# Later sines, squares summed on GpSimd, joined gate weights and paired bias blocks in a hybrid decoder trunk

## The chip, the cores and the metric

The kernel runs on one core of one Trainium2 chip. The metric is the device time of one execution in microseconds, lower is better. The engines are named as the profile names them: PE (TensorE, with PEld for its weight loads), DVE (VectorE), ACT (ScalarE), POOL (GpSimd) and SP (SyncE, which here only issues transfers).

## What is computed

The reference is a trunk of two layers over 512 tokens of width 2048, all in float32. Each layer normalises its input, multiplies it with one combined input projection, feeds the slices to three mixers, gates each, and adds the output projection:

```python
for layer in range(DEPTH):
    xn = rms_norm(h, norm_g[layer])
    mem_kv = mem_n @ mem_w_kv[layer]
    if layer % 2 == 0:   # S5 state-space mixer | forgetting attention | memory attention
        mixed = even_layer(xn, mem_kv, even_w_in[i], s5_lam_re[i], ..., fox_b_f[i])
    else:                # latent attention | sparse attention | memory attention
        mixed = odd_layer(xn, mem_kv, positions, t5_table, odd_w_in[i], ...)
    h = h + (mixed @ w_out[layer]).astype(h.dtype)
return rms_norm(h, final_norm_g)
```

Four pieces matter here. The S5 mixer turns its parameters into a complex decay (`mag * cos(li * dt)`, `mag * sin(li * dt)`) and a factor divided by `lr * lr + li * li`. The forgetting attention has eight forget gates, `log_sigmoid(f_logit + b_f)`, whose logits are eight columns of the input projection. The latent attention normalises two latents of 512 rows: `rms_norm(c_q, g_cq)` and `rms_norm(c_kv, g_ckv)`, which needs the sum of squares over 512 channels for each token. The sparse attention adds a position bias, `t5_table[bucket(distance)]`, to its scores.

## The kernel before, in words

All large products are one list of jobs (`plan`), worked through in order by five instruction streams that are written out by hand and meet only at semaphores. A job is cut into chunks of 512 columns and a chunk into slots of two contraction tiles. For each slot SP loads 512 KB of weights into one of four buffers `wraw` (line 175; it may do so once DVE is done with the slot four before), ACT rounds them to the matmul's type (`act_slot`, line 188), DVE computes what rounding lost (`dve_slot`, line 192), and PE multiplies: high by high, high by low and low by high, three matmuls for each tile and bank (`pe_part`, line 223). So a slot of a full job is 24 matmuls of 512 columns. The ring `wsp` has four slots as well: ACT may convert slot n once PE is done with slot n - 4. Results of a chunk stay in PSUM banks 0 to 3; ACT copies them to `stage` and stores them (`act_evac`, line 303, store at line 343). That evacuation stands in ACT's order after three slots of the next chunk have been converted, and the next chunk's first matmul waits for the banks.

The jobs at the start are memk0, memv0, memk1, memv1 (keys and values of the memory, from `mem`), then E0, E1 and E2 (the even layer's input projection), then GLU. The memk jobs have 256 token columns. E2 is the job of the eight forget-gate columns: its slot is six matmuls whose stationary operand is 128x8. Small work is hooked in between slots: `hook(s)` runs after slot s on each engine.

**The start.** POOL loads the rows of `x` (line 2348) once the first job's transposes are done, then the S5 parameters (`pool_prep_loads`, lines 596 to 603), and runs a long chain of small steps on them (`pool_prep`, lines 611 and 614). In the middle POOL waits for two sines from ACT (`act_prep_sin`, lines 694 and 695) and one reciprocal from DVE (`dve_prep_den`, line 699). ACT and DVE come to these after the conversions of memk1; both stand ahead of the conversions of memv1. PE transposes the results in chunk 1 of E0 (`pe_prep`, line 706). Meanwhile the transposes of x's normalised rows (`pe_tile`, line 472), their scaled copies by ACT (`act_tile`, line 388) and low parts by DVE (`dve_tile`, line 457) are hooked into memk1 and memv1.

**The forget gates.** E2's bank is evacuated after three slots of GLU have been converted. The logits go to DRAM, back to SBUF (`flS`), and through `act_forget` and `dve_forget`, which stand after GLU's conversions.

**The attention sequences.** `Seq` lays the softmax units of a layer (`seq_scores`, `seq_max`, `seq_exp`, `seq_norm`, ...) in steps x, with the matmuls of the output projection filled in between, and `splits` says at which step ACT and DVE convert which slot of that projection.

**The position bias.** The odd layer's bias is built in 32 blocks n while job O1's chunks 1 to 4 run: DVE compares (`dve_t5_ind`), PE multiplies after slot n (`pe_t5`, lines 1897 and 1898), ACT copies (`act_t5_row`), POOL stores (`pool_t5_out`). A block is twelve matmuls with 32 stationary columns each, going to the four partition groups of one bank, three over the same columns, and one 128x128 matmul with an identity that adds the mask. The block's width is 128, 256, 384 or 512 columns, eight blocks of each.

**The latents' squares.** In chunk 6 of O1, ACT squares eight tiles (`act_c`, line 2022), and PE sums each over its partitions with a matmul of ones, two after each of the slots 2 to 5 (`pe_c`, line 2068, float32). ACT's third square waits for the first of these matmuls.

## Time and profile before

| | us |
|---|---|
| median of three runs | 2368.56 |
| lowest and highest | 2366.68, 2369.6 |
| the profiled execution | 2363.92 |
| its span in the profile | 2362.2 |
| PE busy in the span | 2305.3 |
| DVE, ACT, POOL busy | 997.5, 826.4, 374.1 |

The page cuts the span into 40 slices, and its row of the granted clock shows 9 (full) in all but the second. 345.6 MB are moved at 146 GB/s on average. A row of the timeline gives the start and the length of a run of like instructions, their count, and in brackets how long the engine had sat idle before it and who ended that.

### The profile page before, as it was taken

The page shows a single profiled execution, that of the slowest core. Times are in us where ns is not written, and L with a number is a line of the kernel's source. Part 1 is how long each engine was busy: PE and PEld are TensorE (multiplying, and loading weights), DVE is VectorE, ACT ScalarE, POOL GpSimd, SP SyncE. Part 2 cuts the span into 40 slices and gives each one's busy share as a digit, 9 for nine tenths or more (in the row PEclk, how much of TensorE's full clock was granted, in tenths as well). Part 3 has the DMA queues.
Part 4 walks back from the last instruction along what each step waited for, and adds up shares of the span by engine and source line. Part 5 has one row for each costly group of instructions (what it writes and reads, how often), then busy time and mean ns, then how long its engine had stood idle before and what let it go on. Part 6 is the DMA issues. An engine that isn't in the chain of part 4 may idle for free.

```text
span 2362.2 us, 30631 instructions
## 1 busy us (share of the span) xinstructions
PE 2305.3 (98%) x11817; PEld 1873.8 (79%) x11817; DVE 997.5 (42%) x1862; ACT 826.4 (35%) x1468; POOL 374.1 (16%) x629
## 2 busy tenths in 40 slices
PE   7899999999999999999999999999999999999998
PEld 6788888888888877888877777788888866778887
DVE  4533444544432246553353442351121345666534
ACT  5433323333332434432342222322222443455323
POOL 2814111111110011210010001000000154121100
PEclk9899999999999999999999999999999999999999
DMA  8544434444345245654344446345442664454532
GB/s 278 183 127 143 124 110 111 115 125 117 106 124 190 72 140 196 203 178 141 98 147 136 129 140 220 111 121 156 138 121 71 220 222 148 153 181 140 205 116 97
DMA packets 165610, 345.60 MB, mean 146 GB/s; under 512 B 20743, under 2 KB 31319, under 8 KB 163043
## 3 DMA queue, kind: packets, MB, share of 16 engines
q1 hardware_dynamic: 106944, 188.51, 26.5%
q0 software_dynamic: 29840, 98.42, 13.2%
q10 hardware_dynamic: 28691, 56.82, 6.6%
q8 instruction: 91, 1.49, 0.3%
q14 instruction: 44, 0.36, 0.0%
HBM read 279.88 MB, written 63.82 MB: 145 GB/s over the span
## 4 chain that ended last, share of the span: by engine, by line
PE 93%; POOL 2%; DVE 1%; issue 1%; ACT 1%; DMA 1%; SPq 0%; DVEq 0%; ACTq 0%; POOLq 0%
PE PS L223 75%; PE PS L1583 3%; PE PS L2212 2%; PE PS L1572 1%; PE PS L2084 1%; PE PS L271 1%; POOL S L614 1%; PE PS L2109 1%; PE PS L1013 1%; PE PS L1009 1%; PE PS L472 1%; POOL S L611 1%; PE PS L1897 1%; PE PS L1332 1%; PE PS L2105 1%
## 5 line engine op out<-in xcount | busy, mean ns | idle before, releaser
L223 PE MATMUL PS<-A,wsp 128*128 128x512 f32 (+1 forms) x5232 | 1175.4, 384 | 2.5 <-ACT stage L303 1.2
L223 PEld LDWEIGHTS PS<-A,wsp 128*128 128x128 f32 x5232 | 946.4, 187 | 199.0 <-issue 3.7
L192 DVE TENSOR_TENSOR wsp<-wraw,wsp 128x1024 fp32r<-128x1024 f32 (+2 forms) x366 | 435.8, 1192 | 1114.3 <-ACT wsp L188 1113.1
L223 PE MATMUL PS<-wsp,A 128*128 128x512 f32 x2976 | 765.4, 402 | 15.5 <-DVE wsp L192 12.4
L188 ACT ACTIVATE wsp<-wraw 128x1024 fp32r<-128x1024 f32 (+2 forms) x366 | 374.2, 1025 | 996.4 <-PE PS L223 960.3
L223 PEld LDWEIGHTS PS<-wsp,A 128*128 128x128 f32 x2976 | 542.3, 190 | 120.0 <-DVE wsp L192 13.1
L303 ACT ACTIVATE stage<-PS 128x512 f32<-128x512 f32 (+1 forms) x150 | 87.0, 586 | 131.4 <-PE PS L223 131.2
L1619 ACT ACTIVATE S<-PS 128x256 f32<-128x256 f32 (+3 forms) x160 | 63.1, 394 | 129.8 <-PE PS L1572 128.9
L1583 PEld LDWEIGHTS PS<-S 128*128 128x128 f32 x640 | 93.4, 192 | 12.0 <-issue 2.4
L1627 ACT ACTIVATE S<-PS,stats 128x256 f32<-128x256 f32 (+3 forms) x160 | 74.8, 468 | 74.1 <-DVE stats L1664 61.7
L1583 PE MATMUL PS<-S 128*128 128x128 f32 x640 | 95.5, 276 | 1.2 <-issue 1.1
L1572 PE MATMUL PS<-ident,S 128*128 128x128 f32 x336 | 64.4, 277 | 2.3 <-ACT S L1619 2.2
L1572 PEld LDWEIGHTS PS<-ident,S 128*128 128x128 f32 x336 | 45.0, 148 | 20.7 <-issue 10.5
L1664 DVE CUSTOM_DVE_ANT_0 PS<-PS,S 128x512 f32<-128x512 f32 (+4 forms) x80 | 34.9, 437 | 44.1 <-PE PS L1465 23.1
L1914 POOL DMA_DIRECT2D biasD<-S x32 | 17.5, 548 | 226.6 <-ACT S L1908 218.8
L388 ACT ACTIVATE A<-PS,gcol 128x512 fp32r<-128x512 f32 (+1 forms) x48 | 27.6, 613 | 61.9 <-PE PS L472 61.9
L457 DVE SCALAR_TENSOR_TENSOR A<-PS,gcol,A 128x512 fp32r<-128x512 f32 (+1 forms) x48 | 30.1, 657 | 44.2 <-ACT A L388 43.8
L797 POOL COPY S<-S 64x64 f32<-64x64 f32 x32 | 11.9, 401 | 216.6 <-PE PS L959 216.1
L1885 DVE TENSOR_SCALAR S<-S 128x128 bf16<-128x128 f32 (+3 forms) x128 | 40.6, 382 | 0.0
L1678 DVE TENSOR_SCALAR S<-S,stats,gtm 128x32 f32<-128x32 f32 (+4 forms) x96 | 38.3, 399 | 4.1
L810 POOL DMA_DIRECT2D kD<-S x64 | 33.6, 554 | 32.7 <-DVE S L907 29.6
L815 POOL DMA_DIRECT2D S<-kD x64 | 33.6, 534 | 12.9 <-DMA kD<-S 12.8
(326 smaller groups left out, 1741.1 us busy)
## 6 DMA issues: line engine op xcount, KB each, us to landing
wraw<-in_even_w_in_dram SPq DMA_DIRECT2D x112, 512.0 KB, 3.7
wraw<-in_odd_w_in_dram SPq DMA_DIRECT2D x88, 512.0 KB, 3.6
wraw<-in_w_out_dram SPq DMA_DIRECT2D x80, 512.0 KB, 3.7
wraw<-in_mem_w_kv_dram SPq DMA_DIRECT2D x32, 512.0 KB, 4.7
yO<-stage ACTq DMA_DIRECT2D x12, 1024.0 KB
yE<-stage ACTq DMA_DIRECT2D x10, 1024.0 KB
S<-yO POOLq DMA_DIRECT2D x36, 256.0 KB, 3.6
hA<-stage ACTq DMA_DIRECT2D x8, 1024.0 KB
```

Source lines behind the costliest of these rows:

```text
L188: nc.scalar.activation(wsp[:, q, 0, :, 0:j["cols"]], wraw[:, q, :, 0:j["cols"]], ACT.Copy).then_inc(w_hi, 1)
L192: nc.vector.tensor_tensor(wsp[:, q, 1, :, 0:j["cols"]], wraw[:, q, :, 0:j["cols"]], wsp[:, q, 0, :, 0:j["cols"]].bitcast(F32), ALU.subtrac ...
L223: mm = nc.tensor.matmul(dst, lhs, rhs, start=(s == 0 and kk == 0 and i == 0), stop=(s == j["spc"] - 1 and kk == 1 and i == 2))
L303: nc.scalar.activation(stage[0:rows, f, 0:n], PS[0:rows, f, 0:n], func, scale=scale).then_inc(banks_free, 1)
L1572: mm = nc.tensor.transpose(PS[:, 6, j_ * P:j_ * P + P], seqP[x % 4][:, j_ * P:j_ * P + P], ident[:, :])
L1583: mm = nc.tensor.matmul(PS[:, 7, i * P:i * P + P], u["v"](j_), seqT[x % 2][:, j_ * P:j_ * P + P], start=(j_ == 0 and u["first"]), stop=(j_ ...
L1619: nc.scalar.activation(seqT[x % 2][:, 0:n], PS[:, 6, 0:n], ACT.Copy).then_inc(a_ev, 1)
L1627: nc.scalar.activation(seqP[c][:, 0:w], PS[:, 4 + x % 2, 0:w], ACT.Exp, bias=stats[:, 4 + c:5 + c], scale=-1.0 if u["bias"] is not None el ...
L1664: nc.vector.tensor_tensor_reduce(bank, bank, u["bias"], -1.0, 3e38, ALU.add, ALU.min, accum_out=top).then_inc(a_mx, 1)
L1678: nc.vector.tensor_scalar(p, p, stats[:, 12 + c:13 + c], u["gate"], ALU.mult, ALU.mult).then_inc(a_nr, 1)
L1885: nc.vector.tensor_scalar(indS[n % 4][j_][:, 0:w], poskS[:, 0:w], atS[:, 4 * n + j_:4 * n + j_ + 1], None, ALU.is_le).then_inc(t5_ind, 1)
L2212: return nc.tensor.matmul(bank[:, 0:w], nsaQ[r][:, i * P:i * P + P], keys[which][:, 0:w], start=True, stop=True)
```

## The change

- **Start.** POOL waits for x's row block 1 before it issues the S5 parameter loads. `act_prep_sin` and `dve_prep_den` move from behind memk1's conversions to behind those of E0's chunk 0.
- **Forget gates.** The low halves of the eight weight columns are put beside the high halves (columns 8 to 15 of one operand), so that one matmul yields both products; the slot falls from six matmuls to four, the job from 48 to 32. The result has 16 rows, stored and loaded as two groups of eight, which DVE adds (`f_part`) before ACT's `act_forget` may start.
- **Latents.** ACT writes the first square of each latent to `sqA[g]` and the others to two buffers; POOL adds them up (`pool_c_squares`, six additions, behind `pool_w1(1)` in its order and ahead of `pool_w2`); PE sums each latent with one matmul, after slots 4 and 6. Two matmuls of ones instead of eight.
- **Bias blocks.** `pe_t5` does two blocks after each odd slot instead of one after each slot; the identity matmul is cut into four of 32 columns. ACT's row copies come one slot later.
- **Sequences.** The conversions in `splits` begin two steps later (at step 3 instead of 1).

```diff
@@ dve_slot
-            nc.vector.tensor_tensor(wsp[:, q, 1, :, 0:j["cols"]], wraw[:, q, :, 0:j["cols"]],
+            low = wsp[:, q, 0, :, 8:16] if j is E2 else wsp[:, q, 1, :, 0:j["cols"]]
+            nc.vector.tensor_tensor(low, wraw[:, q, :, 0:j["cols"]],
@@ new, in place of pe_chunk(pe, E2, 0)
+        def pe_forget_gates(pe):
+            pe.wait_ge(banks_free, E2["first_free"][0])
+            for s, n, q, r, early in chunk_slots(E2, 0):
+                pe.wait_ge(w_lo, n + 1)
+                for kk in range(2):
+                    kt = 2 * s + kk
+                    for low in (kt > 0, kt == 0):
+                        rows, ap = (8, E2["lo"]) if low else (16, E2["hi"])
+                        mm = nc.tensor.matmul(PS[0:rows, 0, :], wsp[:, q, 0, kk, 0:rows], A[:, ap + kt, :], start=(kt == 0 and not low),
+                                              stop=(kt == KD - 1 and not low))
+                mm.then_inc(slot_used, 1)
@@ act_forget
-            act.wait_ge(fin_, 32)
+            act.wait_ge(f_part, 1)
@@ dve_forget
             dve.wait_ge(fin_, 32)
+            nc.vector.tensor_tensor(flS, flP[:, 0], flP[:, 1], ALU.add).then_inc(f_part, 1)
+            dve.wait_ge(f_part, 1)
@@ Seq
-                self.splits, at = {}, 0
+                self.splits, at = {}, 2
@@ pe_t5
-        def pe_t5(pe, n):
...
+        def pe_t5(pe, n0):
+            for n in (n0, n0 + 1):
...
+                for i in range(3):
+                    for j_ in range(4):
+                        nc.tensor.matmul(bank[32 * j_:32 * j_ + 32, 0:w], dB[i], indS[n % 4][j_][:, 0:w], start=(i == 0), stop=False)
                 for j_ in range(4):
-            nc.tensor.matmul(bank[:, w - P:w], identB, mixB[:, 112 - 16 * g:240 - 16 * g], start=False, stop=True).then_inc(t5_pe, 1)
+                    rows = slice(32 * j_, 32 * j_ + 32)
+                    mm = nc.tensor.matmul(bank[rows, w - P:w], identB[:, rows], mixB[:, 112 - 16 * g:240 - 16 * g], start=False, stop=True)
+                mm.then_inc(t5_pe, 1)
@@ act_c
-                    if k >= 2:
-                        act.wait_ge(ss_pe, k - 1)
-                    nc.scalar.activation(sqS[k % 2], cS[:, k, :], ACT.Square).then_inc(sq_ok, 1)
+                    g, i = k // 4, k % 4
+                    if 3 * g + i - 1 >= 2 and i:
+                        act.wait_ge(sq_added, 3 * g + i - 2)
+                    nc.scalar.activation(sqS[(3 * g + i - 1) % 2] if i else sqA[g], cS[:, k, :], ACT.Square).then_inc(sq_ok, 1)
+        def pool_c_squares(pool):
+            for g in range(2):
+                for i in range(1, 4):
+                    pool.wait_ge(sq_ok, 4 * g + i + 1)
+                    if i > 1:
+                        pool.wait_ge(sq_added, 3 * g + i - 1)
+                    nc.gpsimd.tensor_tensor(sqA[g], sqA[g], sqS[(3 * g + i - 1) % 2], ALU.add).then_inc(sq_added, 1)
@@ pe_c
-            if 2 <= s < 6:
-                if s == 2:
...
+            if s in (4, 6):
+                g = s // 2 - 2
...
+                pe.wait_ge(sq_added, 3 * g + 3)
+                nc.tensor.matmul(PS[:, 6 + g, :], ones[:, :], sqA[g], start=True, stop=True).then_inc(ss_pe, 1)
@@ gpsimd
+            pool.wait_ge(rows_in[1], 16)
             pool_prep_loads(pool)
...
-            pool.dma_start(flS, yE[7168:7176, :]).then_inc(fin_, 16)
+            pool.dma_start(flP, yF.rearrange("g r t -> r g t")).then_inc(fin_, 16)
...
             pool_w1(pool, 1)
+            pool_c_squares(pool)
@@ scalar (and the like for dve_prep_den on vector)
-                if n_ == 2:
-                    act_prep_sin(act)
             act_chunk(act, E0, 0, pend, lambda s: act_early(act, 4, s))
+            act_prep_sin(act)
...
-lambda s: act_t5_row(act, 8 * c + s - 13) if 0 <= 8 * c + s - 13 < 32 else None)
+lambda s: act_t5_row(act, 8 * c + s - 14) if 0 <= 8 * c + s - 14 < 32 else None)
@@ tensor
-            pe_chunk(pe, E2, 0)
+            pe_forget_gates(pe)
...
-                pe_chunk(pe, O1, c, lambda s: pe_t5(pe, 8 * (c - 1) + s))
+                pe_chunk(pe, O1, c, lambda s: pe_t5(pe, 8 * (c - 1) + s - 1) if s % 2 else None)
```

## Rows read from the trace of the kernel before

**Rows 1.** The page: busy us, share of the span, instructions of each engine

```profile
PE 2305.3 (98%) x11817; PEld 1873.8 (79%) x11817; DVE 997.5 (42%) x1862; ACT 826.4 (35%) x1468; POOL 374.1 (16%) x629
```

**Rows 2.** Waits of PE, whole span: total us, times, longest us

```profile
PE PS L223 <- DVE wsp L192: 13.4, 3, 8.8
```

**Rows 3.** Timeline of PE, 42 to 112 us: start, length, work, [idle before]

```profile
42.77 13.79 PE L223 MATMUL PS<-wsp,A 128*128 128x512 f32 x60
...
60.17 10.08 PE L223 MATMUL PS<-wsp,A 128*128 128x512 f32 x36 [3.61 <-DVE wsp L192]
...
70.93 14.30 PE L223 MATMUL PS<-A,wsp 128*128 128x256 f32 x117 [0.34 <-ACT stage L303]
...
95.01 0.60 PE L472 MATMUL PS<-ident,S 128*128 128x128 f32 x4
...
104.45 4.66 PE L223 MATMUL PS<-wsp,A 128*128 128x512 f32 x12 [8.84 <-DVE wsp L192]
...
109.30 3.00 PE L223 MATMUL PS<-wsp,A 128*128 128x512 f32 x12
```

**Rows 4.** Windows: stretch, length, engines busy, PEclk, DMA share, GB/s

```profile
60.20:61.00 0.80, 0.80 (x2) 0.71 (x3) 0.00 (x0) 0.55 (x2) 0.40 (x2) 0.51 1.04 381
```

**Rows 5.** Timeline of ACT and POOL over the same stretch

```profile
85.71 0.69 ACT L388 ACTIVATE A<-PS,gcol 128x512 fp32r<-128x512 f32 x1 [2.19 <-PE PS L472]
...
98.80 0.31 ACT L694 ACTIVATE S<-S 32x128 f32<-32x128 f32 x1 [11.10 <-POOL S L611]
...
103.76 1.15 ACT L303 ACTIVATE stage<-PS 128x256 f32<-128x256 f32 x4
...
120.12 0.52 POOL L611 TENSOR_SCALAR S<-S 32x128 f32<-32x128 f32 x1
```

**Rows 6.** Timeline, PE's transposes of S5 parameters in chunk 1 of E0

```profile
188.35 0.68 PE L706 MATMUL PS<-ident,S 32*128 32x32 f32 x8
```

**Rows 7.** DMA queues, 40 to 44 us: packets, MB, share of 16 engines

```profile
q0 software_dynamic: 201, 1.52, 96.8%
```

**Rows 8.** DMA queues, 48 to 52 us

```profile
q0 software_dynamic: 126, 0.39, 53.7%
q1 hardware_dynamic: 128, 0.23, 34.9%
```

**Rows 9.** Timeline, PE early in the second attention sequence

```profile
2010.28 0.49 PE L2212 MATMUL PS<-A 128*128 128x128 f32 x2 [2.50 <-ACT S L1627]
```

**Rows 10.** Groups of PE by shape, 837 to 848 us: busy, mean ns

```profile
L223 PE MATMUL PS<-A,wsp 128*8 128x512 f32 x48 | 11.0, 389 | 0.0
```

**Rows 11.** Timeline, 847 to 889 us, all engines

```profile
847.20 1.06 ACT L188 ACTIVATE wsp<-wraw 128x1024 fp32r<-128x1024 f32 x1 [0.53 <-DMA wraw<-in_s_w_glu_dram]
...
848.16 0.57 ACT L303 ACTIVATE stage<-PS 8x512 f32<-8x512 f32 x1
...
848.88 43.77 PE L223 MATMUL PS<-A,wsp 128*128 128x512 f32 x192 [0.99 <-DVE wsp L192]
...
886.16 2.35 DVE L192 TENSOR_TENSOR wsp<-wraw,wsp 128x1024 fp32r<-128x1024 f32 x2
```

**Rows 12.** Windows, 842 to 844 us, columns as in rows 4

```profile
842.00:844.00 2.00, 2.00 (x10) 0.79 (x9) 0.33 (x2) 0.22 (x1) 0.55 (x1) 1.00 1.04 363
```

**Rows 13.** Chain that ended last, 1495 to 1525 us: start us, us, what

```profile
1499.34 5.49 PE PS L223 x24
...
1504.83 1.72 PE PS L2068 x4
```

**Rows 14.** The same chain, a stretch of plain matmuls

```profile
1520.96 70.77 PE PS L223 x312
```

**Rows 15.** The same chain at a block of 512 columns, 1417 us

```profile
1417.38 0.76 PE PS L1897 x12
...
1418.30 5.54 PE PS L223 x24
```

**Rows 16.** Line 1897: idle of PE's weight loads before it (us, times)

```profile
  issue: 11.3, 32
```

More of the change, by code:

```diff
@@ L301, in act_evac @@
                 n = j["n"] if j["mode"] == "F" else COLS
-                rows = min(P, j["cols"])
+                rows = 16 if j is E2 else min(P, j["cols"])
                 nc.scalar.activation(stage[0:rows, f, 0:n], PS[0:rows, f, 0:n], func, scale=scale).then_inc(banks_free, 1)
@@ L1886, in dve_t5_ind @@
                                         ALU.is_le).then_inc(t5_ind, 1)
-        def pe_t5(pe, n):
-            w, g = (n // 8 + 1) * P, n % 8
-            bank = PS[:, 4 + n % 4, :]
-            pe.wait_ge(t5_ind, 4 * n + 4)
-            if n >= 4:
-                pe.wait_ge(t5_row, 2 * (n - 3))
-            for i in range(3):
+        def pe_t5(pe, n0):
+            for n in (n0, n0 + 1):
+                w, g = (n // 8 + 1) * P, n % 8
+                bank = PS[:, 4 + n % 4, :]
+                pe.wait_ge(t5_ind, 4 * n + 4)
+                if n >= 4:
+                    pe.wait_ge(t5_row, 2 * (n - 3))
+                for i in range(3):
+                    for j_ in range(4):
+                        nc.tensor.matmul(bank[32 * j_:32 * j_ + 32, 0:w], dB[i], indS[n % 4][j_][:, 0:w], start=(i == 0), stop=False)
                 for j_ in range(4):
-                    nc.tensor.matmul(bank[32 * j_:32 * j_ + 32, 0:w], dB[i], indS[n % 4][j_][:, 0:w], start=(i == 0), stop=False)
-            nc.tensor.matmul(bank[:, w - P:w], identB, mixB[:, 112 - 16 * g:240 - 16 * g], start=False, stop=True).then_inc(t5_pe, 1)
+                    rows = slice(32 * j_, 32 * j_ + 32)
+                    mm = nc.tensor.matmul(bank[rows, w - P:w], identB[:, rows], mixB[:, 112 - 16 * g:240 - 16 * g], start=False, stop=True)
+                mm.then_inc(t5_pe, 1)
         def act_t5_row(act, n):
@@ L1924, in build @@
         rrS = [PS[:, 6 + r, :] for r in range(2)]
+        sqA = [S[:, 10240 + 512 * r:10752 + 512 * r] for r in range(2)]
+        sq_added = sem("sq_added")
         w2S = S[:, 4096:4608].rearrange("p (k h d) -> p k h d", k=2, h=2)
@@ L2061, in pe_c @@
         def pe_c(pe, s):
-            if 2 <= s < 6:
-                if s == 2:
+            if s in (4, 6):
+                g = s // 2 - 2
+                if g == 0:
                     pe.wait_ge(t5_row, 64)
-                for k in (2 * s - 4, 2 * s - 3):
-                    pe.wait_ge(sq_ok, k + 1)
-                    nc.tensor.matmul(PS[:, 6 + k // 4, :], ones[:, :], sqS[k % 2], start=(k % 4 == 0), stop=(k % 4 == 3)).then_inc(ss_pe, 1)
+                pe.wait_ge(sq_added, 3 * g + 3)
+                nc.tensor.matmul(PS[:, 6 + g, :], ones[:, :], sqA[g], start=True, stop=True).then_inc(ss_pe, 1)
         W1_AT = (2, 6, 10, 14, 18, 22, 26, 30)
```

14 lines of the change are left out of this document (8 added, 6 removed).

## The prediction, as it was made before the result

> **What bounds the kernel now.** I read the page first: PE is busy for 2305.3 of 2362.2 us [rows 1]. So a part of the change can only pay in two ways: it takes instructions off PE, or it closes one of the few holes in PE's work. The waits of PE say where the holes are: 13.4 us in all go to conversions that came late, 8.8 of them at one place [rows 2]. The timeline of PE shows the places, both at the start [rows 3]. One is a hole of 3.61 us before 60.17 in memv0; the other opens when the transposes at 95.01 end (95.61) and closes at 104.45, in front of memv1. Each is paid twice: 12 matmuls take 4.66 us behind the second and 3.00 a slot later, and 36 take 10.08 behind the first, where 60 took 13.79 (so 8.3) before it. The windows give the reason: right after the first hole the granted clock is 0.51, the 1.2 GHz level of the two [rows 4]. Everywhere else a plain slot follows a plain slot, and a part is worth what it takes out of PE's stream.
>
> **1. The sines.** ACT sat idle for 11.10 us before the first sine at 98.80, because POOL was still preparing the angle; behind the sine stood the conversions of memv1 and the evacuation of memk1 [rows 5]. The change takes this wait out of memv1's way. What is late next? PE's matmuls of memv1 want memk1's first bank, which ACT frees after the scaled copy of the last transposed tile (0.69 us) and one bank's copy (1.15 / 4 = 0.29) [rows 5]. So PE stands still for about 1.0 us after 95.61 and starts at 96.6. One slot (12 matmuls at 13.79 / 60 = 0.23, so 2.8 us) and the transposes (0.60 busy, about 0.45 of PE's time) bring its second slot to 99.8, where before it came at 109.5 (the row at 109.30, less what matmuls overlap) [rows 3]. Gain 9.7 us; 8.8 if the low clock came nonetheless for half its time, 10.5 if the copies run ahead.
>
> The moved work: two sines of 0.3 us with a table load on ACT, one reciprocal on DVE, and the rest of POOL's chain, which took from 98.80 to 120.64, 22 us, partly waiting for DVE [rows 5]. They now come about when PE is in slot 4 of E0's first chunk, near 157 on the old scale; POOL ends by 180 at the latest, and PE wants the result at 188.35 [rows 6]. ACT and DVE are three slots ahead of PE there. Cost nothing; if POOL took 10 us longer than before, the rest would show in full. POOL's later constants load sits behind this chain, and nobody asks for it before the odd layer.
>
> **2. The S5 loads behind x.** The hole before 60.17 is a transfer's. x's rows hold the 16 DMA engines at 96.8% from 40 to 44 us [rows 7], and then the S5 loads take 53.7% of them for only 0.39 MB in 4 us, while SP's weights get 34.9% and 0.23 MB [rows 8]: small pieces are slow, and a 0.52 MB slot that starts there takes many microseconds. The change starts the S5 loads only when x has landed, some 3 to 4 us after the bus is free for weights. In that time at the rate of [rows 7] (1.52 / 4 = 0.38 MB per us) two weight slots land, and these are the two that memv0's hole waited for. So the hole of 3.61 and its 1.8 us of slow clock (10.08 - 8.3) go [rows 3]. But the bytes remain, and the engines were full until about 63: the third slot of memk1, behind which ACT frees memv0's banks, lands near 65.5 by the same sum of bytes. With its conversion (1.06) and a bank's copy memk1 starts at about 67.9, not at 70.93. Gain 3.0 us. Bounds: 5.4 (both costs gone, nothing late) and -1.8 (the new wait of some 2.5 us before memk1 as long as the old, and the clock falls there too). The nearest hole on PE without low clock is 2.50 us [rows 9], so I leave the clock out.
>
> **3. The forget gates.** 16 of 48 matmuls go: 11.0 / 48 x 16 = 3.7 us of PE [rows 10]. Do they reach the end? Behind them GLU starts at 848.88. ACT converts three GLU slots first; the third waited for its transfer (0.53 us) until 847.20, then came the evacuation of E2's bank, 0.57 us, which releases PE [rows 11]. Between 842 and 844 the DMA engines are full, 1.04 at 363 GB/s [rows 12]: they carry these slots as fast as they can, and the store of the previous chunk ahead of them doesn't move. So E2 would end 3.7 us sooner and GLU start almost when it did: I take 0.3 us. PE's hole there grows from 0.99 to about 4.4 us, longer than the one of 3.61 behind which 1.8 us were lost to the clock [rows 3]. Sum -1.5 us. Bounds +3.7 (everything reaches the end) and -3.3 (low clock for twice as long). The new add on DVE puts ACT's gate chain about 2 us later. It ends in GLU's sigmoids and DVE's conversions of the output job, done at 888.5, while PE is in GLU until 892.6 [rows 11]: hidden, with 4 us of cover, of which it takes up to 2.
>
> **4. The latents.** Between 1499.34 and 1506.55 lie 24 plain matmuls and two with ones, which add 1.72 us in the chain [rows 13]; six of the eight go: 6 x 0.86 = 5.2 us. ACT's squares no longer wait for PE but for POOL, which is idle then; its additions are of the size of one ACT copy, PE needs them a slot or more later. Taken at full value; bounds 3.5 (each of PE's two waits 0.9 late) and 5.5.
>
> **5. The bias blocks.** A plain matmul costs 70.77 / 312 = 0.227 us, so 0.443 ns per column [rows 14]. A block of 512 columns costs 0.92 us from 1417.38 to 1418.30, and the 24 matmuls behind it 5.54 instead of 24 x 0.227 = 5.44 [rows 15]: 1.02 us. Its columns are 3 x 512 + 128, or 0.74 us. The rest, 0.28, is not stream: the weight loads sit idle 11.3 / 32 = 0.35 us before each block, with no releaser [rows 16]. I read this as the cost of changing between 128 and 32 stationary columns. Before, each block changes over twice (into it, and from its twelve matmuls to the identity); now a pair does so twice, half as often. Gain 32 x 0.28 / 2 = 4.5 us. Bounds: 5.6 (the whole 0.35 at 16 visits) and -0.9, if the four quarters of the identity run one after the other (3 x 128 columns, 0.17 us, 32 times = 5.4 us) rather than side by side, as the twelve do. If each quarter cost a share of its own as an instruction, it would be at most 0.76 / 12 = 0.063 us [rows 15].
>
> The Trainium skill ("TensorEngine Tiling (Array Packing)", Instruction Overhead) speaks against the quarters: each matmul has about 60 cycles of overhead. At 2.4 GHz that is 25 ns, so 3 x 32 x 25 ns = 2.4 us as an estimate, and by it the gain would be 2.1 instead of 4.5 us. The twelve matmuls of these rows neither show nor exclude it.
>
> DVE's comparisons for even blocks now wait for a pair that ends one slot later, with its next conversion queued behind. PE needs that conversion three slots later, 16 us; wait, comparison and conversion take under 5.
>
> **6. The splits.** Early in the second sequence PE stands still 2.50 us [rows 9] for an exponential whose maximum stood on DVE behind a conversion. Two steps later the pipeline holds more work. I take 2.0 us for this sequence and nothing for the first, where the holes are smaller; bounds -1.2 (one conversion's length, in the way later) and +3.2.
>
> **The sum**: 9.7 + 3.0 - 1.5 + 5.2 + 4.5 + 2.0 = 22.9 us. Against its own time the profiled execution would go from 2363.92 to 2341.0. The median of the runs shown is 2368.56, 4.6 above it, so I forecast 2345.7.
>
> **Rivals.**
> - The gates pay after all: GLU's weights land as much earlier as E2 ends, with no long hole. For it: SP can issue two of the slots sooner. Against: full engines [rows 12]. 3.7 instead of -1.5: 2340.5. Chance 0.15.
> - The S5 loads only move the hole: part 2 brings -1.8 to 0. For it: the bytes are the same. 2348.7 to 2350.5. Chance 0.18.
> - The quarters cost by the piece: for three more in each of 32 blocks, at between nothing and 0.063 us each [rows 15], the middle is 3.0 us, so 2348.7. For it: four issues replace one. Against: the twelve run as densely as their columns. Chance 0.12. (The skill's overhead, named above, would be this case.)
> - The pairs don't pay: the quarters run one by one. 5.4 us dearer, 2351.1. Chance 0.08.
> - The sines' wait only moves into E0: POOL's remaining chain, beginning 60 us later, isn't ready for PE at 188. Then a hole of some 10 us opens there: about 2355. Against: [rows 5, 6]. Chance 0.04.
> - Slower than before: DVE's wait in the pairs starves PE. 14 of the 16 pairs wait (the first two have free buffers). If the lead of three slots were gone and each pair showed a slot's length, 5.5 us, this would cost 77 us: 2423. It decides once each pair costs over 1.6 us, 22.9 / 14. Against it: conversions stand ready long before. Chance 0.02.
> - The forecast: 0.41.
>
> The case of the forecast alone spans 2341 to 2350. The range takes in the gates' case and the pairs' case with the bounds of the small terms: 2338 to 2353. About 0.2% (4.7 us) is what a measurement of this kernel can tell from no change. Faster by more: 0.97; within: 0.01; slower: 0.02.
>
> **What the profile after would show.** PE: no hole in memv0, about 1 us before memv1, its first slot there in 2.8 us; about 2.5 us before memk1. A hole of 4 us before GLU and a granted clock of 0.5 behind it. Two matmuls of ones. The weight loads' idle before line 1897's blocks 16 times, not 32. No wait of 2.5 us early in the second sequence. Wrong I would be above all if the clock behaves otherwise at the three short holes, as each is worth 1.8 us, and if the quarters don't run side by side.

## The result, and the profile after

The changed kernel takes 2345.56 us (median of 4 runs, 2342.57 to 2346.54) where the kernel before, run beside it, takes 2368.55 (2366.68 to 2369.6). The ratio is 0.9903, 95% interval 0.9889 to 0.9916, so it is faster, by 23.0 us (1%). The profiled execution of after is its fastest: 2342.57 us with a span of 2340.9, against 2363.92 and 2362.2 of before; 21.3 us less.

The forecast was 2345.7. Its sum of 22.9 us came out as 21.3, but not all of its terms hold. The table cuts both traces at the same points of PE's work (starts of the same instructions in the timeline of PE), so each row is the time of one stretch:

| stretch of PE's timeline | before | after | gain | forecast | part |
|---|---|---|---|---|---|
| start to memv0 | 42.77 | 42.59 | 0.18 | 0 | |
| memv0 to the next transposes, in memk1 | 42.30 | 43.39 | -1.09 | 3.0 | 2 |
| from there to the S5 parameters' transposes | 103.28 | 93.94 | 9.34 | 9.7 | 1 |
| from there to the last S5 transposes | 549.78 | 549.78 | 0 | 0 | |
| from there to the first causal mask (gates, GLU) | 160.25 | 162.45 | -2.20 | -1.5 | 3 |
| from there to the transposes of the odd layer | 287.09 | 285.42 | 1.67 | 0 | 6 |
| from there to the last bias block | 251.98 | 247.72 | 4.26 | 4.5 | 5 |
| from there to the compression's weights | 154.12 | 149.01 | 5.11 | 5.2 | 4 |
| from there to the last scores | 399.96 | 400.08 | -0.12 | 0 | |
| from there to the last unit of the second sequence | 225.53 | 221.38 | 4.15 | 2.0 | 6 |
| sum | | | 21.30 | 22.9 | |

The last column names the part of the change that the stretch belongs to.

The page of the profile first: PE is busy 15.6 us less than in [rows 1]. Then PE's waits. Those for VectorE's conversions in [rows 2] have left the list's head; in their place PE waits 12.3 us for ScalarE's evacuations, 5.5 at most, and for an exponential of the second sequence (line 2248) 1.7 at most, where it was 2.50 [rows 9].

```profile
PE 2289.7 (98%) x11885; PEld 1874.2 (80%) x11885; DVE 999.6 (43%) x1863; ACT 824.1 (35%) x1468; POOL 376.1 (16%) x635
```
and the waits of PE (us in all, times, longest):

```profile
PE PS L224 <- ACT stage L319: 12.3, 4, 5.5
...
PE PS L2248 <- ACT S L1647: 2.9, 3, 1.7
```

**The start** (timeline of PE; columns as in rows 3). The hole in memv0 is gone, 96 matmuls run through. Another has opened before memk1, 5.51 us.

```profile
42.59 21.95 PE L224 MATMUL PS<-wsp,A 128*128 128x512 f32 x96
...
70.05 16.10 PE L224 MATMUL PS<-A,wsp 128*128 128x256 f32 x120 [5.51 <-ACT stage L319]
...
85.98 0.60 PE L488 MATMUL PS<-ident,S 128*128 128x128 f32 x4
...
97.67 3.01 PE L224 MATMUL PS<-wsp,A 128*128 128x512 f32 x12 [1.14 <-ACT stage L319]
...
100.87 3.00 PE L224 MATMUL PS<-wsp,A 128*128 128x512 f32 x12
```

**What held memk1 up** (timeline of ACT and POOL). ScalarE waits 4.85 and 1.11 us for the weights of memk1's second and third slot, and only then does it empty memv0's banks. The S5 loads, started 9.5 us later, have landed at 67.44, where POOL starts its chain. From 56 to 60 us (columns as in rows 7) they (q0) hold 73.0% of the DMA engines for 0.42 MB, and SP's weights (q1) get 28.5% and 0.22 MB; in the kernel before they held 26.4% (0.32 MB) in the same 4 us, and the weights 65.6% (0.93 MB). The sines come at 150.46, ahead of the transposes at 179.92 [rows 6], which don't wait.

```profile
66.19 1.06 ACT L188 ACTIVATE wsp<-wraw 128x1024 fp32r<-128x1024 f32 x1 [4.85 <-DMA wraw<-in_mem_w_kv_dram]
...
68.36 1.06 ACT L188 ACTIVATE wsp<-wraw 128x1024 fp32r<-128x1024 f32 x1 [1.11 <-DMA wraw<-in_mem_w_kv_dram]
...
69.33 1.06 ACT L319 ACTIVATE stage<-PS 128x512 f32<-128x512 f32 x2
...
67.44 3.48 POOL L627 TENSOR_SCALAR S<-S 32x2 f32<-32x2 f32 x3 [10.99 <-DMA S<-in_s_c_im_dram]
...
150.46 0.31 ACT L710 ACTIVATE S<-S 32x128 f32<-32x128 f32 x1
...
179.92 0.68 PE L722 MATMUL PS<-ident,S 32*128 32x32 f32 x8
```

and the DMA queues of after, 56 to 60 us:

```profile
q0 software_dynamic: 125, 0.42, 73.0%
q1 hardware_dynamic: 114, 0.22, 28.5%
```

**The clock** (windows; columns as in rows 4): the granted clock is 0.50 of full, the 1.2 GHz level, behind this hole and already within the one before GLU.

```profile
70.10:73.00 2.90, 2.90 (x14) 2.90 (x15) 2.90 (x3) 1.35 (x2) 2.73 (x3) 0.50 0.86 285
...
838.00:840.70 2.70, 0.00 (x0) 0.00 (x0) 2.70 (x4) 2.24 (x3) 0.00 (x0) 0.50 0.75 222
```

**Gates and GLU** (timelines of PE and ACT). The gates' 48 matmuls of 11.0 us [rows 10] are 32 of 7.53, but GLU starts only after a hole of 4.82 us, and its 192 matmuls take 45.66 us, the first of them at the low clock, instead of 43.77 [rows 11].

```profile
828.42 7.53 PE L295 MATMUL PS<-A,wsp 128*16 128x512 f32 x32
...
840.76 45.66 PE L224 MATMUL PS<-A,wsp 128*128 128x512 f32 x192 [4.82 <-ACT stage L319]
...
886.26 5.60 PE L224 MATMUL PS<-wsp,A 128*128 128x512 f32 x24
...
840.05 0.57 ACT L319 ACTIVATE stage<-PS 16x512 f32<-16x512 f32 x1
```

**Bias blocks** (the chain of work that ended last, at a pair of 512 columns; and line 1918's idle time of the weight loads). The pair is one visit: 16 idle stretches, 5.6 us, for 32 and 11.3 [rows 16].

```profile
1412.87 11.13 PE PS L224 x48
1424.00 0.76 PE PS L1918 x12
1424.76 0.06 PE PS L1921 x4
1424.81 0.65 PE PS L1918 x12
1425.46 0.06 PE PS L1921 x4
```

```profile
  issue: 5.6, 16
```

**Latents** (same chain): two matmuls with ones are left, 0.86 us each (a matmul with ones counts as two).

```profile
1496.48 0.86 PE PS L2104 x2
...
1508.27 0.86 PE PS L2104 x2
```

### The profile page after: what moved, and what is told of

The parts are those of the page before. It is cut to its first block, busy times and chain, and to the rows that moved or that the text cites. A ratio compares the mean times of both kernels' runs of the same rounds, so it can differ in the third digit from the quotient of the medians.

```text
span 2340.9 us, 30778 instructions
## 1 busy us (share of the span) xinstructions
PE 2289.7 (98%) x11885; PEld 1874.2 (80%) x11885; DVE 999.6 (43%) x1863; ACT 824.1 (35%) x1468; POOL 376.1 (16%) x635
## 4 chain that ended last, share of the span: by engine, by line
PE 95%; DMA 1%; issue 1%; DVE 1%; ACT 1%; SPq 0%; DVEq 0%; ACTq 0%
PE PS L224 77%; PE PS L1603 3%; PE PS L2248 2%; PE PS L1592 2%; PE PS L2120 1%; PE PS L272 1%; DMA wraw<-in_mem_w_kv_dram 1%; PE PS L488 1%; PE PS L1029 1%; PE PS L2145 1%; PE PS L1025 1%; PE PS L1352 1%; PE PS L1918 1%; PE PS L1774 1%; PE PS L1002 1%
## 5 line engine op out<-in xcount | busy, mean ns | idle before, releaser
L224 PE MATMUL PS<-A,wsp 128*128 128x512 f32 (+2 forms) x5184 | 1163.7, 385 | 11.5 <-ACT stage L319 11.2
L224 PEld LDWEIGHTS PS<-A,wsp 128*128 128x128 f32 (+1 forms) x5184 | 946.0, 189 | 205.4 <-issue 12.0
L1905 DVE TENSOR_SCALAR S<-S 128x128 bf16<-128x128 f32 (+3 forms) x128 | 40.7, 382 | 50.7 <-PE PS L1921 50.7
L1698 DVE TENSOR_SCALAR S<-S,stats,gtm 128x32 f32<-128x32 f32 (+4 forms) x96 | 38.3, 399 | 4.3 <-DVE stats L1694 0.2
```

Of the source, the lines that this page charges most:

```text
L224: mm = nc.tensor.matmul(dst, lhs, rhs, start=(s == 0 and kk == 0 and i == 0), stop=(s == j["spc"] - 1 and kk == 1 and i == 2))
L1698: nc.vector.tensor_scalar(p, p, stats[:, 12 + c:13 + c], u["gate"], ALU.mult, ALU.mult).then_inc(a_nr, 1)
L1905: nc.vector.tensor_scalar(indS[n % 4][j_][:, 0:w], poskS[:, 0:w], atS[:, 4 * n + j_:4 * n + j_ + 1], None, ALU.is_le).then_inc(t5_ind, 1)
```

## The experiments

All start from the changed kernel and alter what their diff shows. Medians come with the ratio to the kernel before, run beside them. That interval is about 0.0015 to either side, 3.6 us, so a single term is read from the traces, where one execution stands for each kernel. Three stretches repeat there within 0.1 us wherever no edit touches them (549.78, 93.9 and 285.4 us). Others do not: the scores' stretch takes 399.94 to 400.88 us, and the bias blocks' 246.97 to 248.11 in the kernels that have them as changed.

### The S5 loads without the wait

```
-            pool.wait_ge(rows_in[1], 16)
             pool_prep_loads(pool)
```

> The changed kernel without GpSimd's wait for x ahead of the S5 loads; all else as changed. Theory: the wait only moves PE's hole. With it gone the loads take the transfers from 48 us on again, memv0 stands still some 3.6 us and loses 1.8 us to the low clock, as in the kernel before, while memk1 starts almost without a hole (0.9 us or less) where the changed kernel stands 5.5 us and loses 1.9 us. Sum: 1.1 us faster than the changed kernel, so about 2344.5 us, and the second slot of memv1 begins near 99.8 instead of 100.87 us. Rival, the forecast's own view: the wait gains 3.0 us, so this kernel is 3.0 us slower than the changed one, 2348.6 us.

Measured: 2344.0 us, ratio 0.9902 (0.9886 to 0.9919). In the timeline of PE the hole is back in memv0 and memk1 starts with a gap of 0.34:

```profile
59.44 9.91 PE L224 MATMUL PS<-wsp,A 128*128 128x512 f32 x36 [3.38 <-DVE wsp L193]
...
70.04 14.29 PE L224 MATMUL PS<-A,wsp 128*128 128x256 f32 x117 [0.34 <-ACT stage L319]
```

The stretch from memv0 to the next transposes takes 41.90 us, 1.5 less than in the changed kernel's trace, which is what the theory asked for (1.1); the forecast's view is out. The median does not show it: 0.9902 stands beside 0.9903. The median does lie 4.6 us below the 2348.6 of the forecast's view, a little more than the interval.

### The changed kernel again

> The changed kernel once more, unaltered, beside the three others of this group. Theory: the spread from one execution to another sits in two places, the hole before memk1 (memv0's start to the transposes of the next stage took 43.4 to 45.9 us in traces of kernels that are alike up to there) and a fall of the clock near 2035 us that some executions have (2.5 us). So a trace of it lies within 43.4 to 45.9 at the first and 221.4 or 223 to 224 us for the second sequence (first scores' end to the last unit), and its median within 2 us of 2345.6. Rival: the changed kernel's profiled execution was typical, and the differences to the variants are all their own edits: 43.4 and 221.4 us again.

Measured: 2344.01 us (2341.74 to 2345.64), ratio 0.9899 (0.9883 to 0.9914). Its profile is of its slowest execution, where the first one was of the fastest. The timeline of PE:

```profile
71.12 17.11 PE L224 MATMUL PS<-A,wsp 128*128 128x256 f32 x120 [6.64 <-ACT stage L319]
```

The first stretch takes 45.54 us, 2.15 more than in the first trace, by a longer hole (6.64) with a longer fall of the clock. Seven further kernels of this study (the gates both ways, the three on the bias blocks and splits, the sines, the latents) are like the changed one up to there; with its own two, nine traces give 43.39, 43.64, 44.88, 45.26, 45.32, 45.42, 45.54, 45.89 and 46.11 us, mean 45.05. The two traces with the loads ahead of x (before and the one above) have 42.30 and 41.90. So the wait costs 3.0 us by this mean, not 1.1, and the first profile was a lucky one. The times do not bear that size out: the eight executions of the changed kernel average 2344.5 us, the four without the wait 2344.1. Both speak against a gain from the wait; how much it loses, between nothing and 3.0 us, stays open. The second sequence takes 221.39 here, as in the first trace. The fall of the clock did not come, and the theory's second place is shown only by other traces (below).

### memv0's banks emptied earlier

```
-                if s == min(3, j["spc"] - 1):
+                if s == min(at, j["spc"] - 1):
                     pending()
...
-                act_chunk(act, j, 0, pend, lambda s: act_early(act, n_, s))
+                act_chunk(act, j, 0, pend, lambda s: act_early(act, n_, s), at=1 if n_ == 2 else 3)
```

> The changed kernel, but ScalarE empties memv0's banks behind its first conversion of memk1 instead of behind its third. Theory: memk1's hole is one of order. PE waits for the last bank, which stands on ScalarE behind conversions whose weights land late (4.85 and 1.11 us of waiting), while the first slot of memk1 has long been converted. PE then starts memk1 near 65.2 instead of 70.05 us, works on slot 0 until 68.2 and finds slot 1 just converted; the hole is about 0.7 us and the granted clock stays at 1.0. Sum: 4.6 us of the hole and 1.9 us of clock, 6.5 us faster, about 2339.1. Rival: the weights' transfers set the pace; the hole only comes one or two slots later, as long as before, with its low clock: gain under 1 us, 2344.6 to 2345.6.

Measured: 2338.72 us, ratio 0.9882 (0.9866 to 0.9899). Timeline of PE:

```profile
41.70 21.95 PE L224 MATMUL PS<-wsp,A 128*128 128x512 f32 x96
...
64.34 5.97 PE L224 MATMUL PS<-A,wsp 128*128 128x256 f32 x45 [0.34 <-ACT stage L319]
...
79.19 0.60 PE L488 MATMUL PS<-ident,S 128*128 128x128 f32 x4
```

No hole above 0.34 us is left, memk1 starts at 64 us, and no fall of the clock is recorded before GLU's. The next transposes begin 37.49 us after memv0, 5.9 less than in the changed kernel's first trace and 8.1 less than in its second. The weights landed late all the same (ScalarE waits 2.23 us for a slot of memk1 until 68.08); it was the order on ScalarE that turned their lateness into PE's.

### The gates as before

```
-            low = wsp[:, q, 0, :, 8:16] if j is E2 else wsp[:, q, 1, :, 0:j["cols"]]
-            nc.vector.tensor_tensor(low, wraw[:, q, :, 0:j["cols"]],
+            nc.vector.tensor_tensor(wsp[:, q, 1, :, 0:j["cols"]], wraw[:, q, :, 0:j["cols"]],
...
-            pe_forget_gates(pe)
+            pe_chunk(pe, E2, 0)
```

> The changed kernel with the forget gates as before: 48 matmuls, the weights' halves in two operands, one store of 8 rows, no addition on VectorE. Theory: GLU's start is set by the transfers of its weights, so the 16 matmuls fill a hole that is there anyway: GLU starts within 0.4 us of 840.76, the hole before it is about 1 us instead of 4.8, and the clock does not fall to 0.5 behind it, which gives back 1.9 us. Sum: 1.5 to 2.3 us faster than the changed kernel, about 2343.6. Rival: the 16 matmuls are on the path, 3.7 us slower than the changed kernel, 2349.3.

Measured: 2343.81 us, ratio 0.9900 (0.9884 to 0.9917). The timeline of PE has GLU's start behind a hole of 0.83 us and no low clock in its 192 matmuls:

```profile
842.67 43.79 PE L223 MATMUL PS<-A,wsp 128*128 128x512 f32 x192 [0.83 <-ACT stage L318]
```

(This trace is 2.4 us late from memk1 on, so its start is not to be held against 840.76.) From the last S5 transposes to the first causal mask it takes 160.11 us, as before (160.25). Nine traces with the gates in one operand and their evacuation at its old place have 162.45 to 163.76, mean 163.24. The rival is out: with 16 matmuls less this stretch is 2.2 to 3.5 us longer, held against this trace and that of before. A third trace of the old form, the last experiment, has 162.77.

### The gates' bank emptied ahead of GLU's conversions

```
-            act_chunk(act, GLU, 0, lambda: act_evac(act, E2, 0))
+            act_chunk(act, GLU, 0, lambda: act_evac(act, E2, 0), at=0)
```

> The changed kernel, but ScalarE empties the forget gates' bank ahead of its conversions of GLU's weights instead of behind the third. Theory: half of GLU's hole is order. The bank is free at 836.7, the first slot (landed at 836.3) is converted by ScalarE at 837.8 and by VectorE at 838.8, so GLU starts near 838.9 instead of 840.76 us, behind a hole of 3.0 us. If a hole of 3.0 us leaves the clock alone (2.50 did, 3.61 did not) the gain is 1.9 + 1.9 = 3.8 us, 2341.8; if not, 1.9 us, 2343.7. Rival: the later slots of GLU wait for their transfers, so that the end of GLU stays: no gain, 2345.6.

Measured: 2344.17 us, ratio 0.9902 (0.9885 to 0.9918). Timeline of PE:

```profile
840.55 45.14 PE L224 MATMUL PS<-A,wsp 128*128 128x512 f32 x192 [3.57 <-DVE wsp L193]
```

The hole is 3.57 us instead of 4.82, and the 192 matmuls take 45.14 us, between the 45.66 of the changed kernel and the 43.79 without low clock. The stretch takes 160.78, 2.5 less than the mean of the nine. That is most of the loss, not a gain over before. The clock fell all the same, so the second of the expected cases held, 1.7 us by the first trace.

### Pairs with the identity undivided

```
-                for j_ in range(4):
-                    rows = slice(32 * j_, 32 * j_ + 32)
-                    mm = nc.tensor.matmul(bank[rows, w - P:w], identB[:, rows], ...)
-                mm.then_inc(t5_pe, 1)
+                nc.tensor.matmul(bank[:, w - P:w], identB, ...).then_inc(t5_pe, 1)
```

> The changed kernel with bias blocks still in pairs, but the identity's matmul of each block undivided, 128 columns of the array wide. Theory: what costs is the change between 128 and 32 stationary columns, 0.14 us each (0.28 us a block over two). A pair then changes over four times, as two single blocks do, so the stage from O1's start to the last block takes 209.8 us as in the kernel before, not 205.3; 4.5 us slower than the changed kernel, 2350.1. Rival: pairing gains by itself, for instance through fewer waits, and the quarters cost or bring nothing: the stage stays near 205.3 us and the time near 2345.6.

Measured: 2349.67 us, ratio 0.9935 (0.9922 to 0.9948). The chain that ended last, at a pair of 512 columns:

```profile
1416.79 0.76 PE PS L1918 x12
1417.55 0.16 PE PS L1919
1417.71 0.76 PE PS L1918 x12
1418.47 0.16 PE PS L1919
1418.63 10.99 PE PS L224 x48
```

The stretch from the odd layer's transposes to the last bias block takes 250.90 us: 3.2 more than with quarters, 1.1 less than before (the expectation counts from O1's start, a little later). The theory's direction holds and its figure does not: a pair costs 12.83 us here, 12.65 in the change, and two single blocks of before 12.92 (2 x 6.46). So pairing alone brings 0.09 us a pair, and quartering 0.18 on top. The rival has a part of it, then.

### One block a slot, with quarters

```
-            for n in (n0, n0 + 1):
+            for n in (n0,):
...
-                pe_chunk(pe, O1, c, lambda s: pe_t5(pe, 8 * (c - 1) + s - 1) if s % 2 else None)
+                pe_chunk(pe, O1, c, lambda s: pe_t5(pe, 8 * (c - 1) + s))
```

> The changed kernel with one bias block a slot instead of two every second slot, the identity's matmul in quarters as in the change. Theory: again two changes of width a block, so 209.8 us for the stage from O1's start to the last block, 4.5 us slower than the changed kernel, 2350.1; if the quarters had a price by the piece of 0.01 us or more, at least 1 us would stand on top. Rival: the quarters themselves bring the gain: 205.3 us and 2345.6.

Measured: 2352.21 us, ratio 0.9939 (0.9927 to 0.9951). The same chain:

```profile
1413.59 0.76 PE PS L1918 x12
1414.35 0.06 PE PS L1921 x4
1414.40 5.66 PE PS L224 x24
```

The stretch takes 252.94, 5.2 more than in the change and 1.0 more than before. A block costs 6.48 (0.76, 0.06 and 5.66) against 6.46: quarters without pairs bring nothing. The three further instructions of a block come to 0.02 us by these rows, 0.007 each, and to 0.03 by the stretch (1.0 us over 32 blocks, which is no more than that stretch varies), 0.01 each. Both take the changes of width to cost the same in either form.

### The splits from step 0

```
-                self.splits, at = {}, 2
+                self.splits, at = {}, 0
```

> The changed kernel with the conversions of the output jobs' first slots planned from step 0 instead of 2 in both sequences. Theory: the two steps are worth 1.6 us in the first sequence and 2.5 us in the second, where the hole of 2.50 us for an exponential comes back near 1990 us; the rest of the 4.15 us between the two traces was a fall of the clock to 0.5 that came in some executions of either schedule. Sum 4.1 us slower than the changed kernel, 2349.7. Rival: the early fall of the clock belongs to the old schedule: then this kernel shows it again near 2035 us in its profile, and the second sequence alone costs 4.1 us, sum 5.8 us, 2351.4.

Measured: 2351.14 us, ratio 0.9935 (0.9923 to 0.9946). Early in the second sequence, timeline and windows:

```profile
1997.41 0.49 PE L2248 MATMUL PS<-A 128*128 128x128 f32 x2 [2.52 <-ACT S L1647]
```

```profile
2000.00:2003.00 3.00, 3.00 (x18) 2.81 (x16) 0.41 (x3) 0.95 (x3) 0.00 (x0) 0.65 0.02 6
...
2044.00:2050.00 6.00, 5.60 (x24) 4.95 (x23) 4.43 (x14) 2.01 (x8) 0.66 (x1) 0.51 0.63 214
```

The first sequence's stretch is 287.09 us, to the hundredth that of before, and 1.67 more than the change. Two of its holes are those of the kernel before, 0.7 and 0.3 us, both ended by ScalarE; the changed kernel has neither. In the second the hole of 2.5 us is back, and 227.85 us stand against 221.38: 2.5 of hole and 3.9 of low clock, which came twice, behind the hole and 45 us later. The median, 5.6 us over that of the changed kernel, is nearer to the rival's 5.8 than to the theory's 4.1, but the interval holds both. Whether the falls belong to the old schedule stays open. Both traces with it have at least one in this sequence (before: 225.53), but so do five of the twelve with the new one: those of the gates' earlier evacuation, of the single blocks, and three below, with 222.9 to 224.6 us; the other seven have 221.35 to 221.42.

### The sines at their old place

```
+                if n_ == 2:
+                    act_prep_sin(act)
             act_chunk(act, E0, 0, pend, lambda s: act_early(act, 4, s))
-            act_prep_sin(act)
```

(and VectorE's reciprocal in the same way)

> The changed kernel with the two sines and VectorE's reciprocal at their old places, between memk1 and memv1. Theory: part 1 and part 2 are not independent. GpSimd's chain takes 38.3 us from its start to the sines (60.52 to 98.80 us before); with the S5 loads behind x it starts at 67.4 instead of 60.5, so the sines would run at 105.7 us, memv1's first slot at 111.4 and its second at 116.2 instead of 100.87: 15.3 us slower than the changed kernel, 2361. Rival: the parts add up, and only what part 1 gained is lost: 9.4 us, 2355.

Measured: 2356.57 us, ratio 0.9951 (0.9938 to 0.9965), 12.6 us over the changed kernel beside it. Timelines of ACT, PE and POOL:

```profile
67.20 2.27 POOL L627 TENSOR_SCALAR S<-S 32x2 f32<-32x2 f32 x3 [10.52 <-DMA S<-in_s_c_im_dram]
...
102.04 0.31 ACT L710 ACTIVATE S<-S 32x128 f32<-32x128 f32 x1 [13.07 <-POOL S L627]
...
107.69 4.71 PE L224 MATMUL PS<-wsp,A 128*128 128x512 f32 x12 [10.80 <-DVE wsp L193]
```

From the transposes in memk1 to those of the S5 parameters it takes 105.29 us against 93.94, so the sines' place is worth 11.35 us here and not 9.34 (nor 15.3). The two parts do depend on each other, by 2.0 us. I had set the sines at 105.7 from a chain of 38.3 us; it took 34.8 (67.20 to 102.04). The chain is the same 61 instructions in both, but GpSimd is busy with them for 33.19 us before and 29.74 here, and VectorE beside them for 18.59 and 12.52. The traces show which ones are stretched. The chain begins with 24 instructions on 32x2 elements; in all 14 traces that makes 336. The 182 with VectorE idle beside them take 0.18 to 0.24 us, none more; of the 154 that overlap a VectorE instruction, 111 take over 0.5 and up to 1.3 us. The timeline of this trace has one of each:

```profile
78.62 0.18 POOL L627 TENSOR_SCALAR S<-S 32x2 f32<-32x2 f32 x1
...
79.06 1.23 DVE L193 TENSOR_TENSOR wsp<-wraw,wsp 128x1024 fp32r<-128x1024 f32 x1 [1.65 <-ACT wsp L188]
79.16 1.17 POOL L627 TENSOR_SCALAR S<-S 32x2 f32<-32x2 f32 x1
```

So GpSimd's small steps stretch where they meet VectorE's work. The Trainium skill ("GPSIMD Engine Reference", Specifications) has GpSimd share its SBUF interfaces with VectorE and names contention where the latter reads two inputs from SBUF, as its conversions do; the rows agree (1.17 us beside a conversion, 0.18 without). No run varies VectorE's work alone.

### Eight matmuls with ones

```
-            if s in (4, 6):
+            if 2 <= s < 6:
...
-                pe.wait_ge(sq_added, 3 * g + 3)
-                nc.tensor.matmul(PS[:, 6 + g, :], ones[:, :], sqA[g], start=True, stop=True).then_inc(ss_pe, 1)
+                for k in (2 * s - 4, 2 * s - 3):
+                    pe.wait_ge(sq_ok, k + 1)
+                    nc.tensor.matmul(PS[:, 6 + k // 4, :], ones[:, :], sqS[k % 2], start=(k % 4 == 0), stop=(k % 4 == 3)).then_inc(ss_pe, 1)
```

(and the squares and additions with them)

> The changed kernel with eight matmuls of ones on the latents' squares, as before, and no additions on GpSimd. Theory: all six matmuls come back on TensorE at 0.86 us each: the stretch from the last bias block to the first matmul with the compression's weights takes 154.1 us as before instead of 149.0; 5.1 us slower than the changed kernel, 2350.7. Rival: part of the gain was not the matmuls but ScalarE's freedom from waiting for TensorE, or GpSimd's additions cost something elsewhere: more or less than 5.1 by over 0.5 us.

Measured: 2352.35 us, ratio 0.9934 (0.9921 to 0.9948). The chain at two of the eight (each counts as two):

```profile
1496.83 1.72 PE PS L2103 x4
```

The stretch takes 154.26 us against 149.01: 5.25, six matmuls at 0.86 and nothing else of size. The median stands 8.3 us over the changed kernel's; held against the trace of the changed kernel beside it, most of the other 3.2 are a longer first stretch (46.11, the longest of the nine, against 45.54) and a fall of the clock in the second sequence (223.79 against 221.39).

### Both evacuations earlier

> The changed kernel with both evacuations earlier on ScalarE: memv0's banks behind the first conversion of memk1, the gates' bank ahead of GLU's conversions. Theory: the two don't touch each other. memv0's takes away the hole of 5.5 us and its low clock, about 6.5 us by the median of that kernel alone; the gates' brought 1.7 to 2.6 us between the last S5 transposes and the first causal mask (160.8 us instead of 162.5 to 163.4). Sum: about 2336.5. Rival: GLU's start is set by its transfers whenever PE arrives early, so that only the first counts: 2338.7.

The two edits above together (`at=1` for memk1, `at=0` for GLU).

Measured: 2337.44 us, ratio 0.9876 (0.9861 to 0.9891). The stretches are 37.08 and 160.98 us, so both hold beside each other; its trace has two falls of the clock in the second sequence (224.62).

### memv0's earlier evacuation, the gates as before

> The changed kernel with memv0's banks emptied behind ScalarE's first conversion of memk1, and with the forget gates as before the change. Theory: both losses of the change are undone: no hole before memk1 (40.8 us from memv0's start to the next stage's transposes, not 43.4 to 45.9), and 160.2 us instead of 162.5 to 163.4 from the last S5 transposes to the first causal mask. 5.9 + 2.8 = 8.7 us faster than the changed kernel, about 2336, the fastest of all. Rival: the gates' old form gains only where PE comes late, and now PE comes 5 us earlier; then 2338.7, no better than the earlier evacuation alone.

The edit of the first evacuation together with that of the gates as before.

Measured: 2336.62 us (2334.94 to 2337.95), ratio 0.9870 (0.9855 to 0.9885). The fastest of all, 7.4 us under the changed kernel beside it; the version above can't be told from it. Timeline and windows at GLU:

```profile
830.73 1.06 ACT L188 ACTIVATE wsp<-wraw 128x1024 fp32r<-128x1024 f32 x1 [2.24 <-DMA wraw<-in_s_w_glu_dram]
...
835.15 45.40 PE L223 MATMUL PS<-A,wsp 128*128 128x512 f32 x192 [1.88 <-ACT stage L318]
```

```profile
837.00:839.00 2.00, 2.00 (x6) 1.52 (x6) 2.00 (x4) 0.00 (x0) 0.32 (x1) 0.50 0.77 237
```

The first stretch is 38.18 us. The gates' one is 162.77, not the 160.2 that the old form had in two other traces: GLU's first weights came 2.24 us after ScalarE was ready for them, where it waited 1.08 in the trace with the gates alone undone, and the clock fell behind a hole of 1.88 us. So the theory got the first half right, and of the second this trace shows only 0.5 us (162.77 against a mean of 163.24), or 0.7 against the earlier evacuation alone (163.44). What the new gates cost depends on when PE arrives.

## Why the prediction was right, and where it was not

**1, sines: right.** 9.34 for 9.7. PE waited 1.14 us before memv1 for the named evacuation (forecast 1.0), the first slot took its 3.0 us at full clock, and the moved work showed nowhere: the 549.78 us behind it are equal in both kernels. With the sines back the hole is there again (10.80 us). That part 2 delays GpSimd's chain, and so raises what part 1 saves, was not in the sum.

**2, S5 loads: wrong, a loss instead of a gain.** The forecast let two weight slots land first and had memk1 start at 67.9, behind a wait of 2.5 us without low clock. The first half is right: memv0 runs through. The step that failed is the arrival of memk1's slots, taken from "the same sum of bytes" as 65.5. ScalarE got the second slot at 66.19 and the third at 68.36. The bytes were the same, but the S5 loads now held 73.0% of the DMA engines just when these slots were on their way, the slots behind which memv0's banks are freed. The hole became 5.51 us, which exceeds the sum of the two it replaces (3.61 and 0.34), and brought the clock fall that I had left out by the row of 2.50 us [rows 9]. Two sums of the prediction are off beside this. From 65.5 its own terms (1.06 for the conversion, some 0.6 for a bank) give 67.2, not 67.9. And its bound of -1.8 names a hole as long as the old one with the clock fallen, which by its own terms is a gain of about 0. The rival "only moves the hole" was right for the first trace (-1.1); by nine traces the loss is some 3 us and lies below the bound. The medians do not resolve it: with and without the wait they agree.

**3, gates: right in mechanism, too small.** Counted from the last S5 transposes, GLU started 0.3 us later than before, where 0.3 sooner was forecast; the hole and the low clock came as told: -2.2 for -1.5 in this pair of traces, about -3 by the mean of nine, within the bound of -3.3. Where the old form met an early PE (the last experiment) the difference was only 0.5 to 0.7 us. The gates' chain took 2 of its 4 us of cover, as said: VectorE has converted the output job's slots at 884.31, and PE goes on at 886.26 without a stop.

**4, latents: right**, 5.11 for 5.2, and nothing of GpSimd's additions shows.

**5, bias pairs: right in size, the mechanism coarser than told.** 4.26 for 4.5, in a stretch that varies by 1.1 us from trace to trace. The forecast had two equal changes of 0.14 us. The chains split it otherwise. The twelve matmuls take 0.76 us behind a matmul 128 wide and 0.65 behind the quarters, so the way in is 0.11. The identity takes 0.16 whole and 0.06 in quarters, so the way out is 0.10 where the identity pays, and 0.14 where the plain matmuls behind do (11.13 against 10.99 for 48). And each visit to the blocks costs about 0.1 more once, whatever stands in it: 10.99 for 48 plain matmuls where 48 x 0.227 is 10.89. Before, a block paid 0.11, 0.10 and 0.1; a pair in quarters pays 0.11, 0.14 and 0.1 once for two blocks, 0.27 us less, and 16 x 0.27 = 4.3. Neither half of the edit does it alone: pairing brings 1.1 us, quarters alone lose 1.0. That halving two equal costs came to the same sum is in part luck. The Trainium skill ("TensorEngine Tiling (Array Packing)", Key Properties) says that a change of tiling mode drains TensorE, without a price; the traces agree that a change costs, and the rows give 0.10 to 0.14 us for it.

The same page of the Trainium skill (Instruction Overhead) counts about 60 cycles of overhead a matmul; at 2.4 GHz that is an estimate of 25 ns, and by it the gain was 2.1 us. The single blocks with quarters show 7 to 10 ns for each further piece, and 4.26 us were gained, so this case does not bear the rule out for matmuls on separate groups of 32 columns. The recorded rival "by the piece", at up to 0.063 us each, is out with it.

The wait that I had put on VectorE is there (50.7 us over 128 comparisons, line 1905, for TensorE) and starves nobody; the slower rival never came near.

```profile
L1905 DVE TENSOR_SCALAR S<-S 128x128 bf16<-128x128 f32 (+3 forms) x128 | 40.7, 382 | 50.7 <-PE PS L1921 50.7
```

**6, splits: too small.** Nothing was forecast for the first sequence and 1.67 came. Two holes that waited for ScalarE, 0.71 and 0.28 us, are gone, which is 1.0 of it; its other holes (up to 1.06 us, ended by VectorE) stay. The other 0.7 shows in no hole. For the second, 2.0 stands against 2.5 of hole and 1.6 of a clock fall that the profiled execution of before had and that of after had not. The latter is chance, as far as the runs tell.

So the total came out near by luck: parts 2 and 3, together 4.8 us worse than forecast, stood against part 6, 3.8 better. Of the sum, 1.6 us are missing, and they came back in the level, again by chance: I added 4.6 us for the distance of before's profiled execution from its median, and after's has 3.0. The step of the prediction that failed is the arrival of memk1's slots, in part 2, with the clock that it left out there.

## What to carry to other kernels

A transfer moved behind another does not vanish: ask which slot now lands behind it, and which instruction on the converting engine is queued after that slot's wait. An evacuation that frees a bank for work already converted belongs ahead of conversions that may wait for a transfer; here that was worth 5.9 to 8.1 us. Taking matmuls off ahead of a job whose start is set by transfers gained nothing. A chain of small GpSimd steps is timed with what VectorE does beside it. Before one execution's profile gives a hole near a transfer its size, compare several traces of unaltered stretches.

## What was not expected of the hardware

- The granted clock fell to 0.5 at holes of 5.51, 4.82, 3.57, 3.38, 2.52 and 1.88 us, yet not behind the 2.50 us of [rows 9], which is the same hole as the one of 2.52. A hole of 4.6 us ahead of the odd layer, which both kernels have and the prediction does not name, brought it in all 14 traces.
- In 7 of 14 traces it fell in the second sequence, nine times in all. Five falls came around two holes of 0.7 us, 1.6 us apart, with a third of 0.4 to 0.9 close behind; the changed kernel's trace has these holes (2032 to 2037 us) and no fall. Three came at a hole of 1.7 us that all 14 traces have. One came behind the 2.52. The length of a hole alone does not tell.
- One fall there cost PE between 1.6 and 2.5 us (222.99 and 223.87 against 221.38).
- Two executions of one kernel differ by 2.15 us in a stretch where transfers of two queues meet, and by less than 0.1 us where they don't (549.78 and 549.79).
- The change of the array's column width shows in the chain as 0.10 to 0.14 us, whichever matmul comes behind it.
- GpSimd's smallest steps take 0.18 to 0.24 us beside an idle VectorE and up to 1.3 us beside a busy one.
